# Block inverse of the recurrence: the second head's transpose in the other half of the partitions, products over four quarters of the array

## What is computed

```
sa    = einsum('bhvk,bhk->bhv', state, a_t)          # a_t = -kk, b_t = kk * a
state = state * w_t[:, :, None, :] + sa[..., None] * b_t[:, :, None, :] + v_t[..., None] * k_t[:, :, None, :]
y_t   = einsum('bhvk,bhk->bhv', state, r_t)
```

## Time and profile before

| | us |
|---|---|
| median of 3 runs | 943.59 |
| the three runs | 943.55, 943.59, 945.46 |
| the profiled execution, own time | 945.24 |
| its span, first to last instruction | 943.3 |
| TensorE busy in it | 915.4 (97%) |
| VectorE busy | 641.0 (68%) |
| ScalarE busy | 465.8 (49%) |
| mean granted TensorE clock | 0.996 |

### The profile page before, as it was taken

The page is one execution under the profiler, slowest core; times in us unless marked ns, Lnnn a source line. Parts: engine busy times, 40 slices in busy tenths (PEclk is TensorE's granted clock), DMA queues, the critical chain, the costliest instruction groups (busy, mean ns, idle before and its releaser), DMA issues. The chain is left out here.

```text
span 943.3 us, 21248 instructions
## 1 busy us (share of the span) xinstructions
PE 915.4 (97%) x8634; PEld 873.8 (93%) x8634; DVE 641.0 (68%) x935; ACT 465.8 (49%) x731; POOL 116.1 (12%) x134
## 2 busy tenths in 40 slices
PE   6999999999999999999999999999999999999988
PEld 6988999999999988889999999999999887899988
DVE  6985866666565766567666656676976576556775
ACT  6564544444443565554444444459534543544452
POOL 1002200000121000040000016630025100000000
PEclk9999999999999999999999999999999999999999
DMA  9532555554555522154555445663524442234541
GB/s 347 182 135 90 179 179 178 178 178 152 175 180 207 171 97 90 46 179 159 186 190 179 150 155 183 225 217 131 179 91 156 91 115 58 91 98 140 172 174 46
DMA packets 22979, 144.52 MB, mean 153 GB/s; under 512 B 2920, under 2 KB 3176, under 8 KB 9088
## 3 DMA queue, kind: packets, MB, share of 16 engines
q1 hardware_dynamic: 21600, 140.26, 42.9%
q0 software_dynamic: 1168, 3.23, 2.0%
q10 hardware_dynamic: 144, 0.06, 0.0%
HBM read 142.47 MB, written 1.06 MB: 152 GB/s over the span
## 5 line engine op out<-in xcount | busy, mean ns | idle before, releaser
L510 PE MATMUL ps<-XH,hi 128*128 128x256 f32 x1304 | 374.9, 287 | 7.9 <-DVE XL L2097 3.6
L511 PE MATMUL ps<-XL,hi 128*128 128x256 f32 x1304 | 370.3, 284 | 0.0
L512 PE MATMUL ps<-XH,lo 128*128 128x256 f32 x1304 | 370.2, 284 | 0.0
L510 PEld LDWEIGHTS ps<-XH,hi 128*128 128x128 f32 x1304 | 251.4, 193 | 14.1 <-issue 12.3
L1860 DVE TENSOR_TENSOR lo<-raw,hi 128x1024 fp32r<-128x1024 f32 (+1 forms) x212 | 245.3, 1198 | 23.5 <-ACT hi L1316 9.5
L511 PEld LDWEIGHTS ps<-XL,hi 128*128 128x128 f32 x1304 | 251.5, 193 | 0.1
L512 PEld LDWEIGHTS ps<-XH,lo 128*128 128x128 f32 x1304 | 251.6, 193 | 0.0
L510 PE MATMUL ps<-HH,hi 128*128 128x256 f32 x576 | 165.3, 287 | 10.1 <-DVE HL L1875 9.2
L511 PE MATMUL ps<-HL,hi 128*128 128x256 f32 x576 | 163.8, 284 | 0.0
L512 PE MATMUL ps<-HH,lo 128*128 128x256 f32 x576 | 163.7, 284 | 0.0
L1316 ACT ACTIVATE hi<-raw 128x1024 fp32r<-128x1024 f32 (+1 forms) x110 | 108.5, 987 | 34.8 <-DMA raw<-in_down 18.6
(11 more groups left out here) (375 smaller groups left out, 1213.9 us busy)
## 6 DMA issues: line engine op xcount, KB each, us to landing
raw<-in_wide SPq DMA_DIRECT2D x107, 1024.0 KB, 4.9
raw<-in_down SPq DMA_DIRECT2D x32, 704.0 KB, 4.0
BI<-bias_table POOLq DMA_DIRECT2D x16, 128.0 KB, 4.3
raw<-in_wide SPq DMA_DIRECT2D x2, 512.0 KB, 6.8
MEM<-in_mem SPq DMA_DIRECT2D x2, 512.0 KB, 7.1
X<-in_x SPq DMA_DIRECT2D x1, 1024.0 KB, 13.7
WG<-in_group SPq DMA_DIRECT2D x1, 768.0 KB, 16.8
out<-X SPq DMA_DIRECT2D x3, 256.0 KB, 2.4
```

The lines of the kernel that those rows point to most:

```text
L510: nc.tensor.matmul(dst, wh, xh, start=first, stop=False, skip_group_check=True)
L511: nc.tensor.matmul(dst, wh, xl, start=False, stop=False, skip_group_check=True)
L512: return nc.tensor.matmul(dst, wl, xh, start=False, stop=last, skip_group_check=True)
```

## The change

The second head of each pair (hh 1) keeps MM and YM with the chunks' halves of the partitions exchanged: what belongs to par is in half 1 - par. AM, NN and the results stay where they were. With this, level_y's matmuls for head 1 use rows par and columns 1 - par of the array, and level_n's product for NN uses rows 1 - par and columns par. A new function `four` issues, for each q, head 0 par 0, head 0 par 1, head 1 par 0, head 1 par 1, with head 0 into bank A_ and head 1 into bank B_. Only A_ is claimed, and its semaphores stand for both. Level_y uses columns 0 to 255 of both banks, level_n columns 256 to 511. Level_n's product for MM still goes through `every`.

Banks 6 and 7 become one PSUM tensor, `both`, and A_, B_, C_ are now banks 6, 7 and 3, so VectorE reads both banks in one instruction for YM and for NN.

MM of head 1 can't be masked out of AM any more, since it lies in other partitions. `grams(g, 0)` therefore starts with 8 matmuls for head 1 alone (rows 64 to 127 of the array, columns 1 - par) into bank C_, and VectorE masks that straight into MM of head 1; the operation L2462 covers head 0 only. In the second half of apply the loops run in the order q, hh, par. The same products are computed as before.

```diff
-        ps = [... for i in range(8)]
+        ps = [... for i in range(6)]
+        both = ctx.enter_context(nc.psum_tensor("ps67", [P, 2, 512], F32))
+        ps += [both[:, 0, :], both[:, 1, :]]
...
-        TOK_BANK = (LOG1, TR, OUT1, TR)
-        GRAM_BANKS = ((LOG0, OUT0), (LOG1, TR), (LOG1, TR))
+        NA, NB, NC = OUT0, OUT1, LOG0
+        TOK_BANK = (LOG1, TR, NC, TR)
+        GRAM_BANKS = ((NA, NB), (LOG1, TR), (LOG1, TR))
...
-            A_, B_, C_ = LOG0, OUT0, OUT1
+            A_, B_, C_ = NA, NB, NC
...
+                if wave == 0:
+
+                    claim(C_)
+                    for q in range(4):
+                        for par in range(2):
+                            r = slice((2 * (q % 2) + par) * CHUNK, (2 * (q % 2) + par + 1) * CHUNK)
+                            last = mm(ps[C_][rows_of(1 - par), q * CHUNK:(q + 1) * CHUNK], KK[HALF:P, 2 * g + q // 2, r],
+                                      AI[HALF:P, 2 * g + q // 2, r], q == 0)
+                    last.then_inc(filled[C_], 1)
...
+            def four(col, f, crossed):
+
+                claim(A_)
+                for q in range(4):
+                    c = slice(col + q * CHUNK, col + (q + 1) * CHUNK)
+                    for hh in range(2):
+                        for par in range(2):
+                            r = rows_of(par if hh == 0 or not crossed else 1 - par)
+                            o = rows_of(par if hh == 0 or crossed else 1 - par)
+                            w, x = f(r, hh, q)
+                            last = mm(ps[(A_, B_)[hh]][o, c], w, x, q == 0)
+                last.then_inc(filled[A_], 1)
...
             def level_y(g, lvl):
                 if lvl == 0:
                     pe.wait_ge(inverse_done, g + 1)
-                holds(B_)
-                every(A_, lambda r, hh, q: (AM[r, hh, q, :], NN[r, hh, q, :]))
+                    holds(B_)
+                four(0, lambda r, hh, q: (AM[r, hh, q, :], NN[r, hh, q, :]), False)
 
             def level_n(g, lvl):
-                holds(A_)
-                every(B_, lambda r, hh, q: (MM[r, hh, q, :], YM[r, hh, q, :]))
+                four(T, lambda r, hh, q: (MM[r, hh, q, :], YM[r, hh, q, :]), True)
                 if lvl < 4:
                     every(C_, lambda r, hh, q: (YM[r, hh, q, :], MM[r, hh, q, :]))
...
             def apply(g):
-                holds(B_)
+                holds(A_)
...
-                for hh in range(2):
-                    for q in range(4):
+                for q in range(4):
+                    for hh in range(2):
                         for par, b in ((0, C_), (1, TR)):
...
                 if wave == 0:
-                    for b in GRAM_BANKS[0]:
+                    full(NC)
+                    nc.vector.tensor_tensor(MM[:, 1, :, :], quarters(ps[NC][:, 0:T]), mask("pair_lower", 4),
+                                            ALU.mult).then_inc(taken[NC], 1)
+                    for b in (*GRAM_BANKS[0], NC):
                         dve.wait_ge(taken[b], fills[b])
-                    link(nc.vector.tensor_tensor(flat(MM), flat(AM), mask("pair_lower", 8), ALU.mult))
+                    link(nc.vector.tensor_tensor(MM[:, 0, :, :], AM[:, 0, :, :], mask("pair_lower", 4), ALU.mult))
...
             def level_y(g, lvl):
-                full(LOG0)
-                nc.vector.tensor_tensor(flat(YM), eighths(ps[LOG0][:, :]), mask(f"join{2 << lvl}", 8),
-                                        ALU.mult).then_inc(taken[LOG0], 1)
+                full(NA)
+                nc.vector.tensor_tensor(YM[:, :, :, :], both[:, :, 0:T].rearrange("p h (q c) -> p h q c", q=4),
+                                        mask(f"join{2 << lvl}", 4).unsqueeze(1).to_broadcast([P, 2, 4, CHUNK]), ALU.mult).then_inc(taken[NA], 1)
...
-                full(OUT0)
-                nc.vector.tensor_tensor(flat(NN), flat(NN), eighths(ps[OUT0][:, :]), ALU.add).then_inc(taken[OUT0], 1)
+                full(NA)
+                nc.vector.tensor_tensor(NN.rearrange("p h q c -> p h (q c)"), NN.rearrange("p h q c -> p h (q c)"), both[:, :, T:2 * T],
+                                        ALU.add).then_inc(taken[NA], 1)
```

More of the change, by code:

```diff
@@ L257, in program @@
         late.close()
-        ps = [ctx.enter_context(nc.psum_tensor(f"ps{i}", [P, 512], F32)) for i in range(8)]
+        ps = [ctx.enter_context(nc.psum_tensor(f"ps{i}", [P, 512], F32)) for i in range(6)]
+        both = ctx.enter_context(nc.psum_tensor("ps67", [P, 2, 512], F32))
+        ps += [both[:, 0, :], both[:, 1, :]]
         PROJ, STAT, LOG, TRA, OUTP = ps[0:2], ps[2], ps[3:5], ps[5], ps[6:8]
@@ L1709, in grams @@
             def grams(g, wave):
-                skip(*GRAM_BANKS[wave])
+                skip(*GRAM_BANKS[wave], *((NC,) if wave == 0 else ()))
             def lv(g):
@@ L1717, in level_y @@
             def level_y(g, lvl):
-                skip(LOG0)
+                skip(NA)
             def level_n(g, lvl):
-                skip(OUT0, *((OUT1,) if lvl < 4 else ()))
+                skip(NA, *((NC,) if lvl < 4 else ()))
             def apply(g):
-                full(LOG0)
[L1725 to L1728, removed]
+                full(NA)
+                nc.scalar.activation(WU[:, 0, :, :], ps[NA][:, :].rearrange("p (q c) -> p q c", q=4),
+                                     ACT.Copy).then_inc(taken[NA], 1)
+                skip(NB)
+                for par, b in enumerate((NC, TR)):
                     full(b)
@@ L1734, in chunks @@
             def chunks(g):
-                skip(LOG0, OUT0)
+                skip(NA, NB)
             def sa(g):
-                skip(OUT1, LOG1)
+                skip(NC, LOG1)
             def yt(g):
-                for par, b in enumerate((OUT0, LOG0)):
+                for par, b in enumerate((NB, NA)):
                     full(b)
@@ L2477, in level_n @@
                 else:
-                    dve.wait_ge(taken[OUT0], fills[OUT0])
-                    dve.wait_ge(taken[OUT1], fills[OUT1])
-                full(OUT0)
-                nc.vector.tensor_tensor(flat(NN), flat(NN), eighths(ps[OUT0][:, :]), ALU.add).then_inc(taken[OUT0], 1)
+                    dve.wait_ge(taken[NC], fills[NC])
+                full(NA)
+                nc.vector.tensor_tensor(NN.rearrange("p h q c -> p h (q c)"), NN.rearrange("p h q c -> p h (q c)"), both[:, :, T:2 * T],
+                                        ALU.add).then_inc(taken[NA], 1)
                 if lvl < 4:
-                    full(OUT1)
-                    nc.vector.tensor_tensor(flat(MM), flat(MM), eighths(ps[OUT1][:, :]), ALU.add).then_inc(taken[OUT1], 1)
+                    full(NC)
+                    nc.vector.tensor_tensor(flat(MM), flat(MM), eighths(ps[NC][:, :]), ALU.add).then_inc(taken[NC], 1)
             def apply(g):
[L2487 to L2490, removed]
+                skip(NA)
+                full(NB)
+                nc.vector.tensor_copy(WU[:, 1, :, :], quarters(ps[NB][:, :])).then_inc(taken[NB], 1)
+                skip(NC, TR)
             def decay(g, c):
@@ L2498, in chunks @@
             def chunks(g):
-                full(OUT0)
+                full(NB)
                 nc.vector.memset(ST8[:, 0, :, :], 0.0)
[L2501 to L2504, removed]
+                nc.vector.tensor_tensor(GT[:, 0, :, :], pair(NB, P), mask("eye", 2), ALU.add)
+                full(NA)
+                nc.vector.tensor_tensor(ST8[:, 1, :, :], pair(NA, 0), decay(g, 1), ALU.mult).then_inc(s_ready, 1)
+                nc.vector.tensor_tensor(GT[:, 1, :, :], pair(NA, T), mask("eye", 2), ALU.add)
             def scan(g, c):
-                b, col = ((OUT0, 0), (LOG0, P))[c - 2]
+                b, col = ((NB, 0), (NA, P))[c - 2]
                 dve.wait_ge(scan_done, 2 * g + c - 1)
@@ L2513, in sa @@
             def sa(g):
-                for hh, b in enumerate((OUT1, LOG1)):
+                for hh, b in enumerate((NC, LOG1)):
                     full(b)
@@ L2519, in yt @@
             def yt(g):
-                skip(OUT0, LOG0)
+                skip(NB, NA)
             def gn(g):
```

## The result

| | before | changed |
|---|---|---|
| median of the first 5 runs, us | 945.27 | 939.41 |
| the runs, us | 943.55, 943.59, 945.27, 945.46, 946.96 | 936.23, 939.38, 939.41, 939.47, 939.73 |
| the profiled execution, own time, us | 945.24 | 939.47 |
| its span, us | 943.3 | 937.5 |
| mean granted clock in it | 0.996 | 0.994 |

The changed kernel is faster: ratio 0.9934, 95% interval 0.9920 to 0.9949, that is 6 us. The forecast was 8.6 us and 935.0, and 939.41 lies above the range of 933.0 to 938.6. The direction held, and so did nearly every row the sum was built from. Two things explain the miss: the granted TensorE clock, which the sum left out and which set both its base (943.59 where 945.27 was measured) and the level of the changed kernel's runs, and about 0.8 us of terms that were too large.

A forecast was written before the change was run, and what follows sets the result against it. The stage of the recurrence was taken as bound by TensorE. 10.1 us gained, less 0.75 for added work and 0.8 for waits, gave 8.6 us: 935.0 us against the 943.59 median, range 933.0 to 938.6.

The forecast's parts named there:

- The size of one product: Level_y, level_n's first product and apply's second half: 0.52 us each instead of 0.98 over four quarters, 0.46 gained.
- The floor near 25 ns: Rival: instructions over four quarters start no closer than about 25 ns; 0.80 us per product, 940.6 us, chance 0.04.
- the missing overlap: Rival: products writing one bank from both row halves hold each other; 0.98 us per product stays, 943.4 us, chance 0.05.
- the slower rival: Rival: in the 20 level products each instruction waits for its predecessor; 1.95 us per product, 962.9 us, chance 0.03.
- the two rules of the Trainium skill: Matmuls never start less than about 25 ns apart; different row tiles cannot access one PSUM bank simultaneously.
- The addition: Second heads' extra transposed Gram product, 0.49 us per group, plus 0.13 net VectorE masking; 0.75 us cost for two groups.
- What is late next: Operands late after shorter products: two close YM cases in group 1 and the transpose at 780.76; 0.8 us lost.
- The waits for MB and YM: Transpose at 780.76 waits 2.1 us, not 1.6, losing 0.46; level_n at group 1, level 3 newly waits 0.35.
- Apply: Second half of apply in its new loop order, both groups: 2 × 0.46 = 0.9 us gained.
- The base and the clock: Forecast set against the three-run median 943.59, not the profiled 945.24: 935.0 us; granted clock in the stage read as 1.00.

The follow-up runs named there:

- the second's levels: Changed kernel run again without any edit, beside the kernel before on the same chip: 937.21 us median of 5, ratio 0.9918.
- the three kernels with the change and slot 19 covered: Changed kernel with slot 19's projection ahead of the transposes, alone (934.28 us), with moves for all remaining waits (934.26), or with only the order changes that paid (933.59).
- heads in turn: Changed kernel, but `four` issues all eight calls of head 0, then the eight of head 1: 940.85 us median of 6, ratio 0.9957.
- short wait: Changed kernel, but level_n's product of group 1, level 0 alone issues all of head 0, then head 1: 937.68 us median of 5.
- two by two: Changed kernel, but `four` issues four calls of head 0, then four of head 1, twice: 938.17 us median of 5.
- apply in the old order: Changed kernel, but the loops of apply's second half run as hh, q, par again: 938.92 us median of 6.
- lv: Changed kernel, but slot 22's half unit of projection stands in slot 21, behind the transposes and ahead of level_y: 937.36 us median of 6.
- the kernel before with slot 19 covered: Kernel before the change, with slot 19's projection moved ahead of the transposes: 943.52 us median of 12, ratio 0.9979.
- the changed kernel's third series: Changed kernel run once more without any edit, compared with the kernel before: 938.63 us median of 6, ratio 0.9933.
- before and its repetition: Kernel before the change, and the same kernel run again without any edit: 945.13 us median of 11, ratio 0.9993, in the repetition.

## Why the prediction was right and wrong

**The size of one product: right.** 0.51 us against 0.52 taken. Both row halves writing both banks cost nothing. The floor near 25 ns, the missing overlap and the slower rival are all refuted by the windows above: 32 instructions in 0.51 us are 16 ns each. With them fall, for this layout, the two rules of the Trainium skill that I had set beside the sum ("TensorE: Matmul & The Clock Gate", section "Wait — 56ns, not 53.3ns?", on the distance between matmuls, and "TensorEngine Tiling (Array Packing)", section "Gotcha 1: PSUM Pressure", on row tiles and banks).

**The addition: right.** 0.46 us of TensorE. Group 0 lost 0.09 us up to its first level_y (forecast 0.13), group 1 0.54 (0.62). VectorE's chain of masks is the rows that were forecast, 0.41 and 0.42 us in place of 0.69:

```profile
685.76 0.41 DVE L2485 TENSOR_TENSOR MM<-ps,cmask 128x256 f32<-128x256 f32 x1
686.30 0.42 DVE L2489 TENSOR_TENSOR MM<-AM,cmask 128x256 f32<-128x256 f32 x1
...
808.91 0.68 DVE L2498 TENSOR_TENSOR YM<-ps,cmask 128x512 f32<-128x512 f32 x1
```

The read of two banks for YM takes 0.68 us, as the one-bank read did.

**What is late next: two of three right, one missed.** The waits for MB and YM came at the places named, with 2.03 and 0.28 us. Missed was lv in group 1. It holds for bank TR, and so for ScalarE's copy of PTS, which ended 0.77 us after level_y's start before the change and 0.77 after it. I had checked VectorE's queue for each level_n and for the transposes, but not the banks that lv holds. Level_y's saving of 0.46 us became 0.1 there: 0.35 to 0.4 us lost.

**Apply: the term was too large.** Forecast 2 × 0.46, measured 0.25 and 0.29. The window I took it from began where the first half's last calls and the second half's first ones mix, and part of the second half already ran beside the first in free quarters. The distance from apply to the step after it would have been the row to use. With these four corrections the sum closes: 8.6, less 0.4 for apply and 0.35 for lv, plus 0.1 each for the addition and for the two waits, is 8.0, and 7.97 was measured between executions without a lower clock in the stage.

**The base and the clock: the step that failed.** The step "against the median I predict 935.0 us" took its base from three runs of which two stood at 943.6. That figure was a fast case by luck. The profiled execution, at 945.24, was the usual one: 38 of 54 runs stand at 945 to 946. From there the sum gives 936.6, with the terms that were too large 937.4, and the changed kernel's middle level is 937.2 to 938.0. The prediction noted the 1.65 us between the two figures and did not ask what made it. It read a granted clock of 1.00 in the stage and took it as given for the changed kernel, and no rival was about the clock. The miss of 4.4 us is then, roughly: 1.7 from the base (943.59 for 945.27), 0.7 from the terms, and 2.0 from the third stretch at 1.2 GHz that put four of the first five changed runs at 0.994. The range allowed 1.0 us for scatter and that downwards, and was too narrow on the upper side. Had the first series drawn the second's levels (937.21), the time would have stood inside the range, with the same step missing.

**What stays open.** Whether the change itself makes low-clock runs more frequent. For it: 7 of 16 runs of the changed kernel stood at 0.994, 3 of 54 of before; of the three kernels with the change and slot 19 covered, 1 of 12 did; of the other five with the change and its wait for MB (heads in turn, short wait, two by two, apply in the old order, lv), 9 of 28 stood at 0.994 or below, and one more at 0.995 (939.66) has three stretches in its profile. The profiled executions with a stretch near 779 us are four (the changed kernel's first and second, short wait, apply in the old order), all with TensorE idle for 1.9 or 2.0 us just before it. Against: the kernel before with slot 19 covered, which has neither the change nor that wait, stood there in 3 of 12. The profiles of heads in turn, lv, two by two and the changed kernel's third series idle as long there and kept the full clock, and the stretches at 298, 646 and 916 us, in code that is not changed, come and go as well: before and its repetition show 298 and 915, the changed kernel's repetition 644 and 777, its third profile one at 906 alone. So the idle time there is not enough by itself. All four executions with a stretch near 779 us also had the one near 646, about 133 us earlier. The three that idled as long and lacked both had none at 779, and neither had the three with the one at 646 and slot 19 covered; heads in turn had the one at 646, idled for 1.9 us, and still kept the full clock at 779. The two may belong together, but neither was varied by itself. The experiment meant to shorten it did not, and no profile of the kernel before has been seen with a stretch at 646 us and the 1.6 us wait together.

## What to carry to other kernels

A small f32 matmul holds only its quarter of the array: 64 x 64 products in rotation over four quarters ran at twice the rate of the same products over two, so it is worth a different place in the partitions for one operand if nothing has to be moved for it. Before adding up such gains, look for everything that each following step holds, banks included, and take a term from the distance between two steps rather than from a window where two products mix. Where runs of one kernel stand on levels, sort them by granted clock first and start the sum from the level that most of them have.

## What the runs showed of the hardware

TensorE started 64 x 64 f32 instructions every 16 ns over four quarters (32 in 0.51 us), with both row halves writing disjoint partitions of both banks, and every 30.6 ns over two. It also looks past calls whose quarter is busy: groups of four calls per pair of quarters cost 0.04 us per product (0.67 against 0.63), groups of eight 0.27 to 0.29 us (0.90 against 0.63, 0.91 against 0.62), and with the heads in turn the M product's first instructions started at 691.29 us, ahead of the last of the product in front of it (691.46).

The granted clock fell from 2.4 to 1.2 GHz for a few microseconds at places that differ between executions of one kernel. In the changed kernel's first profile the share of 0.50 stood once behind 2.0 us in which TensorE idled for VectorE (779 us), and once where TensorE was busy for 4.00 of 4.00 us and another execution had the full clock (646 us). Each such stretch cost 1.2 to 1.8 us. One more or less of them is what parts the changed kernel's profiled executions of 935.80, 937.18 and 939.47 us; for 943.6 against 945.5 us before the change only the mean clock of the runs says so.
